# Attention of the last four query tiles with one PSUM bank per unit: scores up to three units ahead, ScalarE's first operation two ahead

## What is computed

```python
# stick-breaking: A[t,s] = sigmoid(z_ts) * prod_{s<j<t} (1 - sigmoid(z_tj)), s < t
z = (jnp.einsum('bthd,bshd->bhts', qb, k) * scale).astype(F32)
ln1m = jnp.where(mask, jax.nn.log_sigmoid(-z), 0.0)
rc = lax.cumsum(ln1m, axis=3, reverse=True)
a = jnp.where(mask, jnp.exp(jax.nn.log_sigmoid(z) + excl), 0.0)
return jnp.einsum('bhts,bshd->bthd', a.astype(v.dtype), v)
# FoX: softmax attention with the cumulative log forget values added to the logits
s = (jnp.einsum('bthd,bshd->bhts', qb, k) * scale).astype(F32)
s = s + jnp.transpose(cb, (0, 2, 1))[..., None] - ck
p = jax.nn.softmax(jnp.where(mask, s, -jnp.inf), axis=-1)
return jnp.einsum('bhts,bshd->bthd', p.astype(v.dtype), v)
```

## Time and profile before

| what | value |
|---|---|
| median of 3 runs | 3687.98 us (3674.41 to 3694.21) |
| the profiled execution's own time | 3678.38 us |
| its span | 3676.8 us |
| TensorE (PE), share of the span | 87% |
| VectorE (DVE) | 37% |
| ScalarE (ACT) | 26% |
| GpSimd (POOL) | 16% |
| units 20 to 39, stick-breaking, layers 0 and 1 | 550.8 to 597.8, 2376.5 to 2424.4 us |
| units 20 to 39, FoX, layers 0 and 1 | 1177.1 to 1224.2, 2996.9 to 3044.9 us |

### The profile page before, as it was taken

How to read it: one execution, slowest core, us unless ns; L and a number is a source line. 1 busy time by engine, 2 the same in 40 slices (tenths; PEclk the granted TensorE clock), 3 DMA queues, 4 the chain that set the end, 5 groups by cost and what they waited for, 6 DMA issues and landing times. The chain is left out here.

```text
span 3676.8 us, 67694 instructions
## 1 busy us (share of the span) xinstructions
PE 3204.2 (87%) x25256; PEld 1989.8 (54%) x25256; DVE 1365.4 (37%) x3002; ACT 950.5 (26%) x1746; POOL 597.8 (16%) x1090
## 2 busy tenths in 40 slices
PE   6999987888998688799989998978889987887998
PEld 4556654555666455444455666545556654554443
DVE  3235086443224444312142350954433244442211
ACT  2012144332224333211020122433322242331110
POOL 0000000444010044400000000004440101452000
PEclk9999988999999799899989999989999997998999
DMA  5011103887120388710120011048861205995102
GB/s 175 18 36 33 50 10 105 265 287 244 38 83 1 117 278 290 249 66 16 46 96 28 28 45 44 1 129 288 284 217 33 72 1 173 295 299 186 57 29 72
DMA packets 268657, 439.67 MB, mean 120 GB/s; under 512 B 48818, under 2 KB 216403, under 8 KB 268339
## 3 DMA queue, kind: packets, MB, share of 16 engines
q1 hardware_dynamic: 205810, 239.96, 20.4%
q0 software_dynamic: 55744, 189.25, 15.6%
q10 hardware_dynamic: 6912, 7.87, 0.6%
HBM read 410.28 MB, written 26.65 MB: 119 GB/s over the span
## 5 line engine op out<-in xcount | busy, mean ns | idle before, releaser
L806 PE MATMUL ps<-W,xT 128*128 128x320 f32 (+7 forms) x5120 | 1482.9, 465 | 11.5 <-DVEq L449 11.5
L806 PEld LDWEIGHTS ps<-W,xT 128*128 128x128 f32 (+1 forms) x5120 | 856.7, 184 | 585.6 <-issue 291.5
L688 POOL DMA_DIRECT2D branch<-in_cache_sb_v_dram x480 | 258.8, 539 | 637.5 <-issue 597.3
L688 POOL DMA_DIRECT2D branch<-in_cache_fox_v_dram x480 | 258.9, 539 | 621.2 <-issue 579.6
L1468 ACT ACTIVATE branch<-ps 128x512 f32<-128x512 f32 x288 | 165.6, 595 | 386.6 <-PE ps L1051 378.2
L1051 PE MATMUL ps<-C,W 128*128 128x128 f32 x1280 | 199.4, 301 | 73.1 <-DMA W<-in_cache_fox_k_dram 26.6
L1051 PE MATMUL ps<-C,branch 128*128 128x128 f32 x1280 | 194.9, 295 | 65.7 <-DMA branch<-in_cache_sb_k_dram 18.0
L1136 PE MATMUL ps<-branch 128*8 128x64 f32 x9920 | 182.2, 234 | 55.9 <-DMA branch<-in_cache_fox_v_dram 27.6
L1073 PE MATMUL ps<-branch,work 128*32 128x512 f32 x896 | 229.9, 631 | 0.8 <-issue 0.2
L1051 PEld LDWEIGHTS ps<-C,W 128*128 128x128 f32 x1280 | 151.0, 151 | 141.0 <-issue 67.4
L1051 PEld LDWEIGHTS ps<-C,branch 128*128 128x128 f32 x1280 | 147.8, 149 | 146.3 <-issue 96.1
(11 more groups left out here) (246 smaller groups left out, 3389.1 us busy)
## 6 DMA issues: line engine op xcount, KB each, us to landing
branch<-in_cache_sb_v_dram POOLq DMA_DIRECT2D x480, 160.0 KB, 4.3
branch<-in_cache_fox_v_dram POOLq DMA_DIRECT2D x480, 160.0 KB, 4.1
W<-in_cache_sb_k_dram SPq DMA_DIRECT2D x248, 160.0 KB, 3.4
W<-in_cache_fox_k_dram SPq DMA_DIRECT2D x248, 160.0 KB
branch<-in_cache_sb_k_dram SPq DMA_DIRECT2D x240, 160.0 KB, 4.2
branch<-in_cache_fox_k_dram SPq DMA_DIRECT2D x240, 160.0 KB, 4.3
W<-in_w_in_dram SPq DMA_DIRECT2D x14, 1280.0 KB, 6.3
W<-in_w_in_dram SPq DMA_DIRECT2D x9, 1536.0 KB, 7.1
```

The lines of the kernel that those rows point to most:

```text
L688: pool.dma_start(ringV[:, g % 2, p * DA:(p + 1) * DA], cache[L, bass.ds(pg, 1)].rearrange("a s h d -> s (a h d)"))\
L806: ins = pe.matmul(out, src[:, k, t * P:t * P + R], W[i % 2][:, k, a:z], start=(k == 0), stop=(k == kc - 1), **place)
```

## The change

For units 20 to 39 (from `LONG` = 20 on, where a unit's logits fit into 512 columns) each unit gets one PSUM bank of the four and one of four half buffers (`place`, `score_place`). A place comes free for unit u when unit u-4 has left it (`same_place`; for units 20 to 23, unit 18 or 19). `upto` gives how far ahead an engine works: one unit before step 19, and from step 19 on three units for the scores on TensorE and two for `first` on ScalarE. VectorE keeps its order.

```diff
@@ -473,6 +473,27 @@
             n = first_half(seg)
             return [(ps[0:ROWS, bank, 0:n], 0, n), (ps[ROWS:P, bank, 0:N - n], n, N)]
 
+        LONG = HA * NT // 2
+
+        def same_place(u):
+
+            return u - 2 if u < LONG else LONG - 2 + (u - LONG) // 2 if u < LONG + 4 else u - 4
+
+        def place(buffer, u, n):
+
+            if u < LONG:
+                return buffer[:, u % 2, 0:n]
+            half = u % 4
+            return buffer[:, half // 2, (half % 2) * 512:(half % 2) * 512 + n]
+
+        def score_place(u, n):
+
+            return bank2(2 * (u % 2), n) if u < LONG else ps[:, u % 4, 0:n]
+
+        def upto(u, short):
+
+            return min(u + (short if u >= LONG - 1 else 1), len(UNITS) - 1)
+
         def weighed(u):
 
             t, i, h = UNITS[u]
@@ -940,10 +961,10 @@
                     a = h // 2 if kind == "sb" else h
                     if u >= 2:
 
-                        pe.wait_ge(att_first[kind], u - 1)
+                        pe.wait_ge(att_first[kind], same_place(u) + 1)
                     for c in range(0, n, 512):
                         w = min(512, n - c)
-                        ins = pe.matmul(ps[:, 2 * (u % 2) + c // 512, 0:w], qT[q, a, t * P:(t + 1) * P],
+                        ins = pe.matmul(score_place(u, n)[:, c:c + w], qT[q, a, t * P:(t + 1) * P],
                                         kT[q, a, c:c + w], start=True, stop=True)
                     ins.then_inc(att_scores[kind], 1)
 
@@ -956,7 +977,7 @@
                     src = att if kind == "sb" else expd
                     for j in range(t + 1):
                         ins = pe.transpose(ps[:, 4 + j // 4, (j % 4) * P:(j % 4 + 1) * P],
-                                           src[:, u % 2, j * P:(j + 1) * P], ident)
+                                           place(src, u, (t + 1) * P)[:, j * P:(j + 1) * P], ident)
                     ins.then_inc(att_turned[kind], 1)
 
                 def weigh(u):
@@ -987,8 +1008,8 @@
 
                 scores(0)
                 for u, (t, i, h) in enumerate(UNITS):
-                    if u + 1 < len(UNITS):
-                        scores(u + 1)
+                    for ahead in range(upto(u - 1, 3) + 1 if u else 1, upto(u, 3) + 1):
+                        scores(ahead)
                     if u >= 1 and UNITS[u - 1][2] in (1, 3, 4):
                         weigh(u - 1)
                     if h == 2 and i >= 1:
@@ -1400,17 +1421,17 @@
                         act.wait_ge(att_scores[kind], u + 1)
                         if u >= 2:
 
-                            act.wait_ge(att_probs[kind], u - 1)
-                        act.activation(sig[:, u % 2, 0:n], bank2(2 * (u % 2), n), ACT.Sigmoid)\
+                            act.wait_ge(att_probs[kind], same_place(u) + 1)
+                        act.activation(place(sig, u, n), score_place(u, n), ACT.Sigmoid)\
                             .then_inc(att_first[kind], 1)
                     else:
                         act.wait_ge(att_max, u + 1)
                         if u >= 2:
-                            act.wait_ge(att_turned[kind], u - 1)
+                            act.wait_ge(att_turned[kind], same_place(u) + 1)
 
                         if h == 0 and i >= 2:
                             act.wait_ge(att_done[kind], i - 1)
-                        act.activation(expd[:, u % 2, 0:n], bank2(2 * (u % 2), n), ACT.Exp,
+                        act.activation(place(expd, u, n), score_place(u, n), ACT.Exp,
                                        bias=small[:, 40 + u % 4:41 + u % 4],
                                        accum_out=small[:, 50 + (t % 2) * HA + h:51 + (t % 2) * HA + h])\
                             .then_inc(att_first[kind], 1)
@@ -1434,8 +1455,8 @@
 
                 first(0)
                 for u, (t, i, h) in enumerate(UNITS):
-                    if u + 1 < len(UNITS):
-                        first(u + 1)
+                    for ahead in range(upto(u - 1, 2) + 1 if u else 1, upto(u, 2) + 1):
+                        first(ahead)
                     to_sbuf(u)
                     if h == 1 and i >= 1:
                         copy_out(t + 1)
@@ -1850,7 +1871,7 @@
 
                     t, i, h = UNITS[u]
                     n = (t + 1) * P
-                    s = sig[:, u % 2, 0:n]
+                    s = place(sig, u, n)
                     r, e = rest[:, 0:n], SEQ - n
                     dve.wait_ge(att_first[kind], u + 1)
                     link(dve.tensor_tensor(s[:, t * P:n], s[:, t * P:n], const("before"), ALU.mult))
@@ -1860,19 +1881,19 @@
                     link(dve.tensor_tensor_scan(prod[:, e:SEQ][:, ::-1], r[:, ::-1], r[:, ::-1], 1.0, ALU.mult,
                                                 ALU.bypass))
                     if u >= 2:
-                        dve.wait_ge(att_turned[kind], u - 1)
-                    dve.tensor_tensor(att[:, u % 2, 0:n], s, prod[:, e + 1:SEQ + 1], ALU.mult)\
+                        dve.wait_ge(att_turned[kind], same_place(u) + 1)
+                    dve.tensor_tensor(place(att, u, n), s, prod[:, e + 1:SEQ + 1], ALU.mult)\
                         .then_inc(att_probs[kind], 1)
 
                 def largest(u):
                     t, i, h = UNITS[u]
                     n = (t + 1) * P
                     dve.wait_ge(att_scores[kind], u + 1)
-                    diag = bank2(2 * (u % 2), n)[:, t * P:n]
+                    diag = score_place(u, n)[:, t * P:n]
                     link(dve.tensor_tensor(diag, diag, const("after_neg"), ALU.add))
                     if u >= 4:
                         dve.wait_ge(att_first[kind], u - 3)
-                    dve.tensor_reduce(small[:, 40 + u % 4:41 + u % 4], bank2(2 * (u % 2), n), AX, ALU.max,
+                    dve.tensor_reduce(small[:, 40 + u % 4:41 + u % 4], score_place(u, n), AX, ALU.max,
                                       negate=True).then_inc(att_max, 1)
 
                 def finish(t):
```

## The result

The changed kernel is slower: 3698.60 us median of 20 runs (3687.80 to 3717.95) against 3683.97 us median of 20 runs of before, ratio 1.0044, 95% interval 1.0030 to 1.0058. That is 14.6 us. The forecast was no change. Three of the kernels further down had one execution each of 5144 to 10747 us, which the ratios leave out.

The account below looks back on a forecast made before the run. FoX was taken as bound by a chain through three engines, stick-breaking tiles 3 to 1 by VectorE. FoX +1.0 and stick-breaking -1.8 gave -0.8 us, forecast 3687.2 us from 3687.98, range 3675 to 3700 us.

Parts of the forecast that it names:

- What bounds FoX: FoX tiles: a chain through three engines, where head 4's exponential waits because VectorE runs `finish` before that head's maximum.
- entry 0: Unit 19, where TensorE issues three units of scores at once: 0 us, bounds -1 and +1 per FoX phase.
- tile 3's late copy: FoX tile 3: ScalarE's copy of unit 21 came 1.2 us late; more lead was to give that back.
- tile 3's round of 1.34: FoX tile 3: unit 23's copy follows one round later, behind head 4's exponential, costing 1.34 us.
- tile 2's 1.0: FoX tile 2: a late copy given back by the longer lead, put at 1.0 us.
- The forecast's -0.8: Sum over the four attention phases: +1.0 us for FoX and -1.8 us for stick-breaking.
- Rival A: FoX tiles shrink to TensorE's busy time as the lead fills it: -18.3 us with stick-breaking, 3669.7 us; chance 0.10.
- Rival B: FoX tiles: the wait for `finish` costs in full, up to 2.6 us per tile; +15, 3703 us; chance 0.10.
- rival C: FoX tile 1: the clock falls a tile earlier, to 1.2 GHz; twice, +8 us, 3695 us; chance 0.06.
- stick-breaking covered by VectorE: Stick-breaking: if the clock falls a tile earlier, VectorE covers most of the slower TensorE work.

Follow-up runs that it names:

- added matmuls: Changed kernel plus matmuls nobody reads, in free bank 5: two per unit in stick-breaking, eight or six at head 3 in FoX; ratio 0.9969 to before.
- before with the same matmuls: Kernel before plus the same unread matmuls in stick-breaking and at head 3 of FoX, without the longer lead; ratio 0.9977 to before.
- stick-breaking is filled: Runs with two unread matmuls per stick-breaking unit; in the kernel before with stick-breaking alone, 3676.97 us against 3685.95, ratio 0.9978.
- `finish` late: Changed kernel with VectorE's `finish` behind the work of head 4 instead of ahead of it, units 20 to 39; ratio 0.9974 to before.
- ScalarE one ahead: Changed kernel with ScalarE's first operation one unit ahead, as before, and scores still three ahead; ratio 1.0002 to before.

## Why the prediction was wrong

*What bounds FoX: right.* The maximum of head 4 waits behind `finish`, and the lead cannot move it. The 2.9 us from the transposes back to the copy of head 2 were forecast as 3.2, the idle piece of TensorE of 2.42 us as 2.5, the wait once per tile came. It was up to 3.5 us long, not some 2.

*The sum: near the measurement while the clock holds, as far as that can be told.* Both kernels run at 1.00 in the first two stretches of FoX. There the forecast has -1.2 us (entry 0, tile 3's late copy) and +0.3 (tile 3's round of 1.34 less tile 2's 1.0), and -0.73 and +0.17 came. Stick-breaking gave 0.2 us in each of its first two stretches, where nothing was to move. For the later tiles there is no clean comparison: with added matmuls the change stands at +0.8 us in the four phases against before as it was, and at -3.3 against before with the same matmuls. The forecast's -0.8 lies between.

*Rival A* did not come: no tile lost 2 us. The rule of the Trainium skill beside it (Perfetto Trace Analysis, Identifying the Most-Contended Engine) has a reservation that the prediction left out: for TensorE the section does not take the busy time of matmuls as the measure, but weight loads and the arithmetic done. Weight loads were 6.88 of 13.50 us, no more than ScalarE's 6.95. *Rival B* had the right place and the wrong price: in the second stretch, at full clock, the wait behind `finish` costs 0.17 us net, not 2.6, as the lead does gain in the first half of the tile.

*The step that failed is rival C, in its chance and its price.* It got 6 in 100, on the ground that "the forecast idles hardly differ". In FoX they did differ: the same text forecast one idle piece of 2.5 us per tile where before had pieces of 1.35 and 1.22 us. The sum of the idle time, 2.23 of 13.50 us, was compared, not how it is spread. So the forecast itself put the clock at nothing. And the price was put at 8 us, FoX only, with stick-breaking covered by VectorE. It was some 18 us, the phases of the changed kernel without and with the added matmuls (219.3 less 201.3), and 5.3 us of the loss against before lie in stick-breaking, where at the lower clock TensorE itself becomes the bound (10.62 of 11.30 us busy, VectorE 8.98), so that the cover is gone. As C was priced too low, 0.92 stood on no change, where the measured change is 0.44% and clear of noise. That 3698.6 lies inside the range, which ended at 3700, is luck: the range was built on three executions of before with a median of 3687.98, 4.0 us above that of twenty. Shifted by that, it would have ended at 3696.

*Left open.* The added matmuls in stick-breaking gain some 9 us that no attention window shows. The span outside the four phases scatters from 3458 to 3484 us between single profiles of the thirteen kernels of the table, so one trace each cannot place 9 us. The mean granted clock of the timed runs points the same way without placing it: 0.930 at the median (0.925 to 0.934) for before, 0.920 to 0.924 for the changed kernel, 0.935 to 0.937 at the median where stick-breaking is filled, and 0.931 for `finish` late, which gains by its order. Also open is what brings the clock down early in stick-breaking, where no idle piece is longer than 0.8 us. That it isn't fixed by the order shows there too: with ScalarE one ahead layer 0 has the same idle pieces as the changed kernel (0.5 to 0.8 us) and keeps its clock some 10 us longer than layer 1.

## What to carry to other kernels

A longer lead does not help a unit whose input waits for something off the loop; it moves that unit's consumer in front of work that was ready. Look in each engine's order for what a moved instruction now stands ahead of, and move the blocker (here `finish`) together with the lead: apart they gave 1.0044 and 0.9996, together 0.9974. Or shorten the lead of the one engine whose order suffers: with ScalarE one ahead the second stretch of FoX took 10.72 us, for 11.96 before and 12.13 with two.

When a change alters how TensorE's idle time is spread, price the clock too: not by the idle sum alone, but also by where a long piece now stands, and with the work behind it at 1.2 GHz, which can make TensorE the bound of a stage that another engine bounded. A long piece is a warning, not the only way there: the clock fell early with pieces of at most 1.3 us too. Some useless matmuls in a free bank tell whether the clock is the cause; put them into the kernel before as well, as here they gained 5.7 us there too.

## What the runs showed of the hardware

Work that nobody needs made this kernel faster: six or eight matmuls of 128 columns per FoX tile (eight are 1.95 us of TensorE time, in an idle piece of 2.4) kept the granted clock at 1.00 for a tile longer, and the two FoX phases went from 57.02 and 57.68 us to 51.60 and 51.64.

The granted clock isn't a function of the code alone: in one execution the same instructions ran at 1.00 in one layer and at 0.50 in the other, with the same tile before them. The phase differed by 5.8 us between the layers for that reason, as much as most of the effects looked for here.
